# A two-layer attention and recurrence block: the output projection in passes of 256, 512, 256 and 256 tokens, each followed by its layer norm, with norm and next modulation in one ScalarE step

## What is computed

```
for l in range(DEPTH):
    shift, scale, gate = split(cond @ w_ada[l] + b_ada[l])
    h  = x  * (1.0 + scale) + shift
    hc = cx * (1.0 + scale_c) + shift_c
    y, yc = mixer(h, hc, ...)              # ends with ... @ w_out
    x = layer_norm(ALPHA * x + gate * y, ln_g[l], ln_b[l])
    if l == 0:
        cx = layer_norm(ALPHA * cx + gate_c * yc, ln_g[l], ln_b[l])
return x
```

## Time and profile before

| | |
|---|---|
| median of 3 runs | 1793.4 us (1789.64 to 1794.16) |
| the profiled execution | 1788.54 us, span 1786.5 us |
| TensorE busy | 1643.3 us, 92% |
| VectorE busy | 640.9 us, 36% |
| ScalarE busy | 566.2 us, 32% |
| GpSimd busy | 82.1 us, 5% |
| chain that ended last | TensorE 71%, issue 16%, VectorE 6%, ScalarE 4% |

### The profile page before, as it was taken

How to read it: one execution, slowest core, us unless ns; L and a number is a source line. 1 busy time by engine, 2 the same in 40 slices (tenths; PEclk the granted TensorE clock), 3 DMA queues, 4 the chain that set the end, 5 groups by cost and what they waited for, 6 DMA issues and landing times.

```text
span 1786.5 us, 25259 instructions
## 1 busy us (share of the span) xinstructions
PE 1643.3 (92%) x9836; PEld 985.8 (55%) x9836; DVE 640.9 (36%) x1401; ACT 566.2 (32%) x1277; POOL 82.1 (5%) x143
## 2 busy tenths in 40 slices
PE   4999999889999999889999888999999899999995
PEld 2476766555656565554554347586655355555442
DVE  2113424421513214331114563134344355554144
ACT  0222222332413324432112342213134365554024
POOL 0000000000000000000011100000000011111111
PEclk7999999989999999999999899999999999999997
DMA  8100021110313023000224310001000000001322
GB/s 344 68 25 24 13 84 60 53 66 31 124 59 131 12 72 119 24 13 27 74 93 154 106 70 36 12 13 37 24 25 24 13 19 7 25 13 39 109 82 100
DMA packets 33348, 108.32 MB, mean 61 GB/s; under 512 B 3536, under 2 KB 5840, under 8 KB 31952
## 3 DMA queue, kind: packets, MB, share of 16 engines
q1 hardware_dynamic: 27792, 97.27, 14.8%
q10 hardware_dynamic: 5440, 9.44, 1.4%
HBM read 97.26 MB, written 9.44 MB: 60 GB/s over the span
## 4 chain that ended last, share of the span: by engine, by line
PE 71%; issue 16%; DVE 6%; ACT 4%; DMA 1%; POOL 1%; ACTq 0%; SPq 0%; POOLq 0%; DVEq 0%
PE proj L888 27%; PE mixed L888 13%; PE proj L871 4%; PE mixed L871 4%; PE mixed L990 3%; PE turned L976 3%; PE scores L1084 2%; PE scores L956 2%; ACT work L1522 2%; PE scores L1110 1%; DMA weights<-in_weights 1%; PE scores L959 1%; PE turned L1121 1%; ACT yT L1522 1%; DVE kvV L1483 1%
## 5 line engine op out<-in xcount | busy, mean ns | idle before, releaser
L888 PE MATMUL proj<-hT,weights 128*128 128x512 f32 (+1 forms) x1376 | 553.9, 549 | 11.5 <-ACT kvV L1522 2.6
L888 PEld LDWEIGHTS proj<-hT,weights 128*128 128x128 f32 x1376 | 256.2, 194 | 236.8 <-issue 226.7
L888 PE MATMUL mixed<-hT,weights 128*128 128x512 f32 (+1 forms) x416 | 175.2, 565 | 1.7 <-ACT kvV L1522 1.7
L888 PE MATMUL proj<-yT,weights 128*128 128x512 f32 x320 | 141.1, 592 | 0.0
L1522 ACT ACTIVATE work<-work,stat 128x640 f32<-128x640 f32 (+8 forms) x144 | 108.8, 755 | 41.7 <-DVE stat L1285 37.9
L888 PEld LDWEIGHTS mixed<-hT,weights 128*128 128x128 f32 x416 | 77.4, 192 | 77.2 <-issue 74.4
L888 PE MATMUL mixed<-yT,weights 128*128 128x512 f32 (+1 forms) x320 | 115.0, 512 | 0.0
L1522 ACT ACTIVATE work<-turned 128x512 f32<-128x512 f32 (+2 forms) x136 | 72.8, 535 | 109.1 <-PE turned L972 98.4
L976 PE MATMUL turned<-consts,work 128*128 128x128 f32 (+4 forms) x656 | 99.8, 279 | 7.9 <-ACT work L1522 7.9
L976 PEld LDWEIGHTS turned<-consts,work 128*128 128x128 f32 (+4 forms) x656 | 74.8, 139 | 54.4 <-issue 33.6
L1379 DVE SCALAR_TENSOR_TENSOR work<-work,turned 128x128 f32<-128x128 f32 (+1 forms) x152 | 53.1, 349 | 142.3 <-PE turned L1121 139.1
(11 more groups left out here) (223 smaller groups left out, 1966.4 us busy)
## 6 DMA issues: line engine op xcount, KB each, us to landing
weights<-in_weights SPq DMA_DIRECT2D x131, 512.0 KB, 3.3
tables<-in_bias SPq DMA_DIRECT2D x8, 1281.0 KB, 7.8
hT<-in_xT SPq DMA_DIRECT2D x8, 640.0 KB, 9.3
work<-in_xT SPq DMA_DIRECT2D x16, 256.0 KB, 3.3
x1T<-yT ACTq DMA_DIRECT2D x8, 512.0 KB, 2.7
work<-x1T SPq DMA_DIRECT2D x16, 256.0 KB, 3.3
out<-yT ACTq DMA_DIRECT2D x8, 512.0 KB, 2.8
tables<-in_tables SPq DMA_DIRECT2D x1, 1792.0 KB, 7.3
```

The costliest lines, as they stand in the source:

```text
L888: last = nc.tensor.matmul(PJ[BANK_OF[u]][:, 0:n], weights[:, w % WBUFS, k, :], src[:, k, t0:t0 + n], start=(k == 0), stop=(k == KT - 1))
```

## The change

The projection's passes and the norms now have one chunk list, `NORMS`: tokens 0 to 255, 256 to 767, 768 to 1023 and 1024 to 1279. Each chunk is a pass of its own over the eight weight tiles (four passes in layer 0, three in layer 1), and its norm runs beside the pass behind it. The running total is added by VectorE. In layer 0, `scale` writes to `yT`, ScalarE makes `hT` from it in one step with the coefficients `blend` (norm and next modulation multiplied out), and `next` then applies ln_g and ln_b in place on VectorE for the spill, which SyncE issues. A gate row's three copies become one, and two projection groups stand between the `rows_turn` steps that were filler of the recurrence.

```diff
+NORMS = [(0, CTX), (CTX, 512), (CTX + 512, 256), (CTX + 768, 256)]
...
     out += [("square_sum", l, ci), ("rstd", l, ci)]
-    for f in range(KT + 1):
-        if f < KT:
-            out.append(("scale", l, ci, f))
-        if f and l == 0:
-            out.append(("next", ci, f - 1))
-    return out
+    out += [("scale", l, ci, f) for f in range(KT)]
+    return out if l else out + [("next", ci, f) for f in range(KT)]
...
-    s += out_projection(0, 0, CHUNKS_ALL[:2])
-    rest = out_projection(0, 1, CHUNKS_ALL[2:])
-    s += rest[:7] + [("column_sum", 0, 0), ("column_sum", 0, 1)] + interleave(norm(0, 0) + norm(0, 1), rest[7:])
+    s += out_projection(0, 0, NORMS[:1])
+    parts = [out_projection(0, ci, NORMS[ci:ci + 1]) for ci in range(1, 4)]
+    s += parts[0][:5] + [("column_sum", 0, 0), ("blend",)] + interleave(norm(0, 0), parts[0][5:])
+    s += parts[1][:5] + [("column_sum", 0, 1)] + interleave(norm(0, 1), parts[1][5:] + parts[2][:8])
+    s += [("column_sum", 0, 2)] + interleave(norm(0, 2), parts[2][8:])
...
-    s += ready[:8] + [("column_sum", 0, 2)] + interleave(norm(0, 2), ready[8:]) + rest
-    s += values("ml", 0)
-    s += [("rows_exp",)]
-    s += [("rows_turn", t, Slot()) for t in range(NT)]
-    fill = project(("ml", 1, "q"), "q", CHUNKS_LAT) + project(("ml", 1, "k"), "k", CHUNKS_ALL)
+    s += ready[:4] + [("column_sum", 0, 3)] + interleave(norm(0, 3), ready[4:]) + rest
+    s += values("ml", 0) + [("rows_exp",)]
+    s += alternate([("rows_turn", t, Slot()) for t in range(NT)], project(("ml", 1, "q"), "q", CHUNKS_LAT))
+    fill = project(("ml", 1, "k"), "k", CHUNKS_ALL)
...
-    s += out_projection(1, 0, CHUNKS_LAT[:1])
-    rest = out_projection(1, 1, CHUNKS_LAT[1:])
-    s += rest[:7] + [("column_sum", 1, 1)] + interleave(norm(1, 1), rest[7:])
-    s += [("column_sum", 1, 2)] + norm(1, 2)
+    s += out_projection(1, 1, NORMS[1:2])
+    parts = [out_projection(1, ci, NORMS[ci:ci + 1]) for ci in range(2, 4)]
+    s += parts[0][:5] + [("column_sum", 1, 1)] + interleave(norm(1, 1), parts[0][5:] + parts[1][:8])
+    s += [("column_sum", 1, 2)] + interleave(norm(1, 2), parts[1][8:])
+    s += [("column_sum", 1, 3)] + norm(1, 3)
...
 SyncE
+                if s[0] == "next" and s[2] % 2:
+                    ci, f = s[1:]
+                    t0, n = NORMS[ci]
+                    sp.wait_ge(*at(("x_after", 0, ci, f)))
+                    sp.dma_start(a["x1T"][f - 1:f + 1, :, t0:t0 + n].rearrange("k p n -> p k n"),
+                                 yT[:, f - 1:f + 1, t0:t0 + n]).then_inc(
+                        *up(f"spilled{ci}", *([("spill", ci)] if f == KT - 1 else []), by=16))
...
 VectorE, out group
+                    if f:
+                        link(V.tensor_tensor(total(t0, n), hT[:, 0, t0:t0 + n] if f == 1 else total(t0, n),
+                                             hT[:, f, t0:t0 + n], ALU.add), ("total", l, f, t0))
...
 VectorE, scale and next
-                link(V.tensor_tensor(h, h, rstd[:, 0:n], ALU.mult), ("scaled", l, ci, f))
+                link(V.tensor_tensor(h if l else yT[:, f, t0:t0 + n], h, rstd[:, 0:n], ALU.mult), ("scaled", l, ci, f))
...
-                dve.wait_ge(*at(("x_after", 0, ci, f)))
-                link(V.tensor_scalar(hT[:, f, t0:t0 + n], yT[:, f, t0:t0 + n], mods[:, 1, 8 + f, w:w + 1],
-                                     mods[:, 1, f, w:w + 1], ALU.mult, ALU.add),
-                     *([("h1", ci)] if f == KT - 1 else []))
+                dve.wait_ge(*at(("h1_made", ci, f)))
+                y = yT[:, f, t0:t0 + n]
+                link(V.tensor_scalar(y, y, col("ln_g", f), col("ln_b", f), ALU.mult, ALU.add), ("x_after", 0, ci, f))
...
 ScalarE, rows_turn and scale
-                for i in range(3):
-                    run(tokc[:, t, i, :].rearrange("p (g r) -> p g r", g=2), src[:, i, :, :], ACT.Copy,
-                        [("proj_free", u), ("rows_turned", t)] if i == 2 else [])
+                run(tokc[:, t, :, :].rearrange("p i (g r) -> p i g r", g=2), src, ACT.Copy,
+                    [("proj_free", u), ("rows_turned", t)])
...
+                if l == 0:
+                    w = 1 if t0 == 0 else 0
+                    run(hT[:, f, t0:t0 + n], yT[:, f, t0:t0 + n], ACT.Identity,
+                        [("h1_made", ci, f)] + ([("h1", ci)] if f == KT - 1 else []),
+                        scale=blend[:, 0, f, w:w + 1], bias=blend[:, 1, f, w:w + 1])
+                    return
```

More of the change, by code:

```diff
@@ L486 @@
          "residual_loaded0", "residual_loaded1", "bias_loaded0", "bias_loaded1"]
-        + ["spilled0", "spilled1", "spilled2", "stored1", "stored2"] + [f"x_loaded{k}" for k in range(KT)] + [f"weight_loaded{i}" for i in range(WBUFS)])
+        + ["spilled0", "spilled1", "spilled2", "spilled3", "stored1", "stored2", "stored3"] + [f"x_loaded{k}" for k in range(KT)] + [f"weight_loaded{i}" for i in range(WBUFS)])
 def build(nc, a, known):
@@ L699, in chunk_no, with chunk_of, norms_of @@
             return [x[0] for x in CHUNKS_ALL].index(t0)
+        def chunk_of(t0):
+            return max(i for i, x in enumerate(CHUNKS_ALL) if x[0] <= t0)
+        def norms_of(t0, n):
+            return [ci for ci, (lo, m) in enumerate(NORMS) if lo < t0 + n and t0 < lo + m]
         def sum_bank(t0):
-            return [SC[:, 0:512], SC[:, 512:1024], TP[0][:, :]][chunk_no(t0)]
+            return (SC[:, 0:512], SC[:, 512:1024], TP[0][:, :], SC[:, 0:512])[norms_of(t0, 1)[0]]
         ada_rows = work[:, 6400:6400 + P]
@@ L726, in tail @@
         def tail(l, ci):
[L728 removed]
+            return (l, ci) == (1, 3)
         def square_bank(ci):
[L731 removed]
+            return (MI, OV, TP[1], MI)[ci]
         def step_before(q, first=0, by=1):
@@ L791, in _ @@
                             if l:
-                                for ci in range(1, 3):
+                                for ci in range(1, 4):
                                     sp.wait_ge(*at(("spill", ci)))
@@ L806, in _ @@
                     sp.dma_start(tables[:, 0:TABLES_W], a["tables"]).then_inc(*up("tables_loaded", ("tables",), by=16))
-            for ci in range(3):
+            for ci in range(4):
                 sp.wait_ge(*at(("spill", ci)))
-            sp.wait_ge(*at(("stored", 1)))
-            sp.wait_ge(*at(("stored", 2)))
+            for ci in range(1, 4):
+                sp.wait_ge(*at(("stored", ci)))
         @block.tensor
@@ L859, in s_mm @@
                     if dest == "gates":
-                        pe.wait_ge(*at(("h1", chunk_no(t0))))
+                        for ci in norms_of(t0, n):
+                            pe.wait_ge(*at(("h1", ci)))
                     if dest == "out" and kind[2] == 0:
@@ L863, in s_mm @@
                             early = early_gate(kind[1], f)
-                            pe.wait_ge(*at(("y_turned", kind[1], f) if early else ("gated", kind[1], f, t0)))
+                            pe.wait_ge(*at(("y_turned", kind[1], f) if early else ("gated", kind[1], f, CHUNKS_ALL[chunk_of(t0)][0])))
                 if dest in ("vt", "vv"):
@@ L1206, in s_mm @@
                     dve.wait_ge(*at(("proj", u)))
-                    dve.wait_ge(*at(("sum", 0, CTX + 512)))
+                    dve.wait_ge(*at(("sum", 0, NORMS[3][0])))
                     link(V.tensor_copy(kvV[:, t0 // P:(t0 + n) // P, :], ps.rearrange("p (t n) -> p t n", n=P)),
@@ L1507, in _ @@
                     "lin_attend": s_lin_attend, "lin_chunk": s_lin_chunk, "lin_out": s_lin_out, "lin_norm": s_lin_norm, "rows": s_rows,
-                    "centre": s_centre, "square_sum": s_square_sum, "scale": s_scale, "next": s_next}
+                    "centre": s_centre, "square_sum": s_square_sum, "scale": s_scale, "blend": s_blend, "next": s_next}
             for s in SCHEDULE:
@@ L1567, in s_mm @@
                 elif dest == "gates":
-                    act.wait_ge(*at(("spill", chunk_no(t0))))
+                    for ci in norms_of(t0, n):
+                        act.wait_ge(*at(("spill", ci)))
                     for k in range(2):
@@ L1732, in _ @@
         def _(pool):
-            def s_mm(kind, dest, t0, n, u, stage, part):
-                if dest != "out" or part != 3:
-                    return
-                l, f = kind[1], kind[2]
-                if f == 0:
-                    return
-                pool.wait_ge(*at(("resid_sum", l, f, t0)))
-                if f >= 2:
-                    pool.wait_ge(*at(("total", l, f - 1, t0)))
-                pool.tensor_tensor(total(t0, n), hT[:, 0, t0:t0 + n] if f == 1 else total(t0, n), hT[:, f, t0:t0 + n],
-                                   ALU.add).then_inc(*up("pool_done", ("total", l, f, t0)))
             def s_ptrans(uid, unit, g):
@@ L1765, in s_ptrans @@
                     *up("pool_done", ("sums_wide", uid)))
-            part = {"mm": s_mm, "ptrans": s_ptrans}
+            part = {"ptrans": s_ptrans}
             for s in SCHEDULE:
```

37 lines of the change are left out of this document (20 added, 17 removed).

## The result

The changed kernel takes 1808.3 us (median of 5, 1805.7 to 1817.8) against 1793.4: a ratio of 1.0097, 95% interval 1.0068 to 1.0126. It is slower by 15 us where 20 us less were forecast. Its profiled execution took 1805.72 us (span 1803.6), 17.1 us more span than before. L904 is now the projection matmul, L862 the column sum, L925 the sum of squares, L915 the tail's squares, L816 the spill, L803 the residual load, L763 the weight load.

What follows compares the result with a forecast made beforehand. TensorE, busy for nearly all of the span, was taken as the bound. Terms -12.9 + 1.0 + 0.9 - 1.6 + 1.4 - 8.5 = -19.7 us gave 1773 us from the median; own range 1767 to 1780, overall 1761 to 1786.

Steps and rivals of the forecast that it cites:

- Old waits of layer 0: Layer 0's projection: TensorE's waits for sums of squares, and the lower clock around them, all go, -23.5 us.
- New waits: Layer 0's projection: new TensorE waits on squares, banks and spills, +10.6 us in pieces of at most 2.5, no clock loss.
- Chunk 3 runs beside wide groups, and the gates wait only for ScalarE's step: none.: End of layer 0: the last chunk's norm adds no new TensorE wait, 0 us.
- Spills ahead of residual loads: Layer 0, SyncE's queue: spills waiting for VectorE delay residual loads, 1.5 us for two groups and 1.1 for the last.
- hidden, with 3.5 us of cover: Narrow groups' residual loop: load landing, ScalarE's scaling and VectorE's add, 1.1 us plus 2.3 landing, fit under 6.92 us.
- rival of starved narrow groups: 40 narrow groups: residual landing grows past 5.8 us; at 8 us 44 us slower, 1817 us; chance 0.04.
- Turning: Gate-row turns between the layers: one ScalarE copy for three, two projection groups woven in, 8.3 us becomes 6.7, -1.6.
- recurrence, 0: Recurrence behind the turns: losing 13.7 us of filler costs 0, bound +14 us.
- the rival that I gave 0.06: Recurrence: it needed its filler, +5 to +14 us, 1787 us at worst; chance 0.06.
- Layer 1 before the tail: Layer 1's projection: waits for squares' sums and one add pushed by ScalarE's scales, 2.0 us for 0.6, +1.4.
- Tail, -8.5: Behind layer 1's last projection group: 23.1 us, column sum starting at E + 5.0; -8.5, bounds -12 and -5.
- The signs: Named for wrong: gaps in every narrow pair, a layer 0 wait above 4 us, or lin_turn's matmuls waiting more in the recurrence.

Runs made afterwards that it cites:

- E2: Changed kernel with only the four spills of the last layer 0 chunk issued from GpSimd: 1798.0 us, 1.0043 of the kernel before.
- E1: Changed kernel with all sixteen layer 0 spills issued from GpSimd's queue instead of SyncE's: 1788.3 us, 0.9987 of the kernel before.
- E5: E1 without ScalarE's scaling of the loaded residuals, the factor folded into the projection's gate: 1767.9 us, 0.9868 of the kernel before.
- E8: Kernel before without ScalarE's scaling of the residuals, nothing else changed: 1788.5 us, 0.9980 of the kernel before.
- E9: Changed kernel without ScalarE's scaling of the residuals, spills left on SyncE: 1788.3 us, 0.9979 of the kernel before.
- E3: Kernel before plus single-copy turns of the gate rows, woven with two query groups taken from the recurrence's filler: 1794.2 us, 1.0019.
- E6: E5 with the two query groups back in the recurrence as filler, single copy of the turns kept: 1763.4 us, 0.9846 of the kernel before.
- E4: Kernel before plus the layer 1 part alone (last chunk split, its totals on VectorE, norms behind passes): 1797.4 us, 1.0035.

## Why the prediction was wrong

The sum said -19.7 us and the span grew by 17.1, so 37 us lie between them. By the medians, four things make up about that much: ScalarE's scaling of the residuals (some 16, taken as hidden), the last four spills (10, taken as nothing), the other twelve (9.7 for 2.6) and the turns with the recurrence's filler (+3.4 for -1.6). Term by term:

- **Old waits of layer 0, -23.5**: right in kind. The three waits for squares and the two shorter ones are gone.
- **New waits, +10.6**: 15.9 in the same stretch, with some 4.6 us of lower clock that I had at nothing (behind the 4.41 us wait the sum of squares and 12 halves take 2.07 and 4.81 us, for 1.02 and 2.75 of such rows at the upper level; the group behind the 3.21 us wait takes 5.11 for 3.62), and 10.1 more in a place where I had none. One by one: the first chunk's squares 1.39 for 1.5, right. The second chunk's 4.41 for 2.5: I added up VectorE's work as if it never waited within a pass, 3.9 us, and it takes 4.4 with the scaling. Bank waits and spills together 5.6 (0.91, 1.47 and 3.21) for 4.4. The third's squares 3.35 for 2.2. A column sum's wait of 1.17 I did not have.
- **"Chunk 3 runs beside wide groups, and the gates wait only for ScalarE's step: none."** This step failed by 10 us (E2: 10.4). I moved the spills past SyncE's residual loads and priced that, but not past its weight loads, and I asked who waits for SyncE, not who waits for the spill: ScalarE, which overwrites what is being spilled.
- **Spills ahead of residual loads, 2.6**: the twelve ahead of residual loads cost 9.7 (E1 against E2), 5.9 us of it in waits and some 1.8 in matmuls at the lower clock.
- **Residuals "hidden, with 3.5 us of cover"**: the landing took 3.2 us (median) for the 2.3 put in, still far below the 5.8 that the cover allowed, but the loop's other half was wrong: ScalarE's 0.42 stands behind squares that wait for VectorE. With layer 1 and the tail this is the largest cost of all, some 16 us (E5, E8, E9), and the step of the prediction that failed most. The rival of starved narrow groups was the only one with a slower kernel, but by landings past 5.8 us and equally in all forty groups; that is not what happened.
- **Turning, -1.6, and recurrence, 0**: together +3.4 (E3) and +4.5 (E6), the rival that I gave 0.06. The turns by themselves came as worked out: 13.8 us with a group of 6.9 among them (1122.70 to 1136.50), 6.9 for the 8.3 of before, -1.4. The recurrence lost 5.5. "The work between its chain steps hardly changes where it waited before" was false.
- **Layer 1 before the tail, +2.8 with the sums and narrow groups**: +8.6 in this execution, +11 to +13 in E1, E2 and E4, by the same loop and the clock. **Tail, -8.5**: -6.4. Its start at E + 5.0 came as worked out (5.03 in the row); the eight squares took 6.8 us for 4.8. The start is late because of the scaling: 1.1 us behind the last group without it (E5). Without the scaling the tail is 19.0 us, 12.6 less than before.
- **Sign**: the mechanisms that should gain do gain. With spills that wait for nobody, no scaling and the filler left where it was, the same norms and passes take 1763.4 us (E6).
- **The signs**: two of those named for being wrong came, a wait above 4 us in layer 0 (4.41 and 8.40) and longer waits for the chain in the recurrence (3.0 for 1.3). Gaps in every pair of narrow groups did not.

Left open: why nearly the same waits in layer 1's projection left TensorE busy there for 114.2, 116.8 or 118.8 us in one execution or another, and how the scaling's loss divides between narrow groups and the total on VectorE.

## What to carry to other kernels

A DMA that is moved to another engine's queue takes two lists with it: what waits ahead of it there, and who waits for its landing; look for an instruction ahead of it that waits for an engine which will itself soon need the landing. When work is cut into shorter pieces, add up the engines' work along the handovers within one piece, not engine by engine: here an operation of 0.4 us per group cost the whole kernel 4 us in wide passes and 20 in the changed one. And an operation that can be folded into a coefficient is worth removing from such a loop before the loop is rearranged.
